# A two-layer block in split precision: the first two weight tiles are split by halves, their products are reordered, and x by token is loaded later

## The chip, the cores and the metric

The kernel runs on one core of a Trainium2 chip. The time is the device time of one execution in microseconds (us), and less is better. The engines are TensorE (PE; its weight loads are listed as PEld), VectorE (DVE), ScalarE (ACT), GpSimd (POOL) and SyncE (SP), which issues nearly all transfers.

## The reference, cut to what matters

The whole program is two transformer-like blocks over 256 tokens of width 2048, all in float32. Only its first step is touched here: a root-mean-square norm of x, and one wide product.

```python
h = rms_norm(x, g_mix_pre[layer])          # x: 256 x 2048
proj = h @ w_in[layer]                     # w_in: 2048 x 9728
aq, ak, av, hq, hf, hi, hg, gate_a, gate_b = jnp.split(proj, split_at, axis=-1)
aq = rotary(aq.reshape(B, S, ATTN_HEADS, ATTN_HEAD_DIM), positions)
```

Everything behind it (windowed attention, a gated recurrence, a feed-forward part, then the second block) works on what comes out of this product.

## The kernel before

**Three products for one.** A float32 product is made of three in the type fp32r: each operand is split into a high part (a copy rounded to fp32r, made by ACT) and a low part (operand minus high part, made by DVE). PE adds up high x high, low weight x high x, and high weight x low x. In the profile the high and low parts of weights are `wh` and `wl` (or `ah` and `al`, when the operand buffers of a later stage are lent for it), those of x by feature are `hh` and `hl`.

**Units, blocks, slots, items.** A unit is a weight of 256 rows by 512 columns (512 KB, 128 x 1024 in the chip's memory: two tiles of 128 x 512). It takes 12 matmuls of 512 columns: two tiles of rows, two halves of the tokens, three products. A block is eight units that add up in one pair of PSUM banks; the blocks `qkv` 0, 1 and 2 are the first three (units 0 to 23). Blocks alternate between two pairs of banks, so block 2 (its first unit is unit 16) can't start before block 0 has been read out of its banks: `unit` waits for `a_ev`, which ACT signals in its stage `q(0)`. An item is one transfer into a landing buffer (`raw` 0 to 3 or four places in `arena`). Units are numbered from 0, and item n is unit n here. A slot is one step of a common timetable, and in slot t PE does unit t.

**What sets the order.** Each engine has a program of its own, written out ahead of time. `drive` walks the slots: in each it does what `AHEAD` has, then the engine's main work (`unit` on PE, `high` on ACT, `low` on DVE), and then lets every stage that `START` has begun go on to its next `yield`, in the order in which they were begun. On DVE, from slot 10 on, the stages come before the main work of the slot. Engines do their lists strictly in order and wait on semaphores. `high` and `low` run ahead of PE: slot 12 of ACT splits units 15 and 16, slot 13 unit 17, slot 14 unit 18.

**The stages that matter here.** `xstats` squares and sums x by token (`X0`, four blocks of 512 columns, two halves of tokens: eight ACT instructions 128 x 512, each followed by a read of its sum), DVE adds the sums up, POOL takes the root, DVE copies it to `R1` and signals `v_r1`. `tables` makes the sine tables for the rotary step (DVE computes angles, ACT takes `Sin`, four times). `lb` prepares a small vector with one `Exp` on ACT. `q(0)` reads block 0 out of its banks on ACT, scaled by `R1` (so it waits for `v_r1`). `Exp` and `Sin` each need an ACT_TABLE_LOAD before them when the table isn't the one loaded.

**Transfers.** SP issues in order: weights (`item`), x by feature (`x_t`, eight pieces of 256 KB), x by token (`x_nat`, four pieces of 512 KB), and three small constants. Units 0 to 7 have buffers of their own from the start.

**The beginning.** PE does 14 matmuls on zeros first. For unit 0 it does its four high products, then the four with the low weight, then the four with low x; unit 1 and all others wait for both low parts before the first matmul.

## Time and profile before

| | |
|---|---|
| time, median of 3 runs | 2183.93 us (2182.58 to 2184.54) |
| time of the profiled execution | 2185.99 us |
| its span in the profile | 2184.2 us |
| mean granted TensorE clock | 0.997 of full speed |
| busy in the span: PE / DVE / ACT / POOL | 2171.8 / 1522.7 / 1109.9 / 47.1 us |
| DMA, mean over the span | 230 GB/s |

The span runs from the first to the last instruction that the profile shows; the profiled execution took 1.8 us more than its span and 2.1 us more than the median. Times inside the trace are counted from the span's start.

### The profile page before, as it was taken

Reading aid. Unit: us, or ns where it says so; the run is one execution under the profiler, and the core shown is the slowest. Engines: PE = TensorE matmul, PEld = TensorE weight load, DVE = VectorE, ACT = ScalarE, POOL = GpSimd, SP = SyncE. Lnnn points to the kernel's source line nnn. Section 1 sums busy time; section 2 is a strip of 40 time slices with the busy share of each in tenths; the row PEclk is TensorE's granted clock in tenths of the full one; section 3 lists DMA queues with packets and bytes.
Section 4 is the critical chain, followed back from the end, with each engine's and each line's share of the span. In section 5 each row is a group of like instructions: output and inputs, shape, how many; then the busy total and the mean of one; then the engine's idle time right before and its main releaser. Section 6 shows DMA issues by size and latency. Waiting matters only on the chain.

```text
span 2184.2 us, 27819 instructions
## 1 busy us (share of the span) xinstructions
PE 2171.8 (99%) x10865; PEld 1799.8 (82%) x10865; DVE 1522.7 (70%) x2026; ACT 1109.9 (51%) x1521; POOL 47.1 (2%) x66
## 2 busy tenths in 40 slices
PE   9999999999999999999999999999999999999999
PEld 7888887888888888888888888887888887888887
DVE  6675479778867777777777778767465577555566
ACT  6676466444446444444443444566465455546452
POOL 0000000100000000000000000000000000000000
PEclk9999999999999999999999999999999999999999
DMA  9544665598886898999999989574564573665573
GB/s 327 169 144 146 193 178 172 173 392 292 281 290 225 300 304 302 311 299 307 305 303 309 305 302 304 180 246 118 146 195 149 165 250 116 172 171 157 156 237 120
DMA packets 243220, 502.87 MB, mean 230 GB/s; under 512 B 17024, under 2 KB 25456, under 8 KB 241936
## 3 DMA queue, kind: packets, MB, share of 16 engines
q1 hardware_dynamic: 239792, 486.20, 68.9%
q0 software_dynamic: 3296, 14.88, 1.9%
q8 instruction: 86, 1.41, 0.3%
q14 instruction: 46, 0.38, 0.1%
HBM read 498.89 MB, written 2.12 MB: 229 GB/s over the span
## 4 chain that ended last, share of the span: by engine, by line
PE 94%; DVE 2%; DMA 2%; ACT 1%; issue 1%; SPq 0%; POOL 0%; DVEq 0%; ACTq 0%
PE bank L959 90%; PE bank L962 4%; ACT arena L1398 1%; DMA raw<-in_w_in 1%; DMA arena<-in_w_in 1%; DVE wl L2015 0%; DMA raw<-in_w_ple_gate 0%; ACT wh L1398 0%; DVE hl L2015 0%; DVE arena L2023 0%; ACT ah L1398 0%; DVE arena L2022 0%; SPq L754 0%; DVE al L2015 0%; SPq L750 0%
## 5 line engine op out<-in xcount | busy, mean ns | idle before, releaser
L1398 ACT ACTIVATE wh<-raw 128x1024 fp32r<-128x1024 f32 (+2 forms) x500 | 520.6, 1043 | 656.1 <-PE bank L959 600.4
L2015 DVE TENSOR_TENSOR wl<-raw,wh 128x1024 fp32r<-128x1024 f32 (+2 forms) x500 | 599.6, 1202 | 343.3 <-ACT wh L1398 341.6
L959 PE MATMUL bank<-wh,hh 128*128 128x512 f32 (+1 forms) x1568 | 617.2, 395 | 4.0 <-DVE wl L2015 3.2
L959 PE MATMUL bank<-wh,hl 128*128 128x512 f32 (+1 forms) x1568 | 605.1, 387 | 0.0
L959 PE MATMUL bank<-wl,hh 128*128 128x512 f32 (+1 forms) x1568 | 604.3, 386 | 0.0
L959 PE MATMUL bank<-wh,ah 128*128 128x512 f32 (+1 forms) x1168 | 456.1, 391 | 0.4 <-ACT ah L1398 0.2
L959 PE MATMUL bank<-wh,al 128*128 128x512 f32 (+1 forms) x1168 | 450.9, 387 | 0.0
L959 PE MATMUL bank<-wl,ah 128*128 128x512 f32 (+1 forms) x1168 | 450.1, 386 | 0.0
L959 PEld LDWEIGHTS bank<-wh,hh 128*128 128x128 f32 x1568 | 294.8, 188 | 63.2 <-DVE wl L2015 4.1
L959 PEld LDWEIGHTS bank<-wh,hl 128*128 128x128 f32 x1568 | 294.2, 188 | 60.5 <-DVE hl L2015 0.5
L959 PEld LDWEIGHTS bank<-wl,hh 128*128 128x128 f32 x1568 | 295.2, 188 | 55.6
L1398 ACT ACTIVATE wh<-arena 128x1024 fp32r<-128x1024 f32 x184 | 195.1, 1061 | 274.2 <-PE bank L959 267.6
L2015 DVE TENSOR_TENSOR wl<-arena,wh 128x1024 fp32r<-128x1024 f32 x184 | 225.0, 1224 | 94.0 <-ACT wh L1398 93.5
L959 PEld LDWEIGHTS bank<-wh,al 128*128 128x128 f32 x1168 | 219.2, 188 | 43.9
L959 PEld LDWEIGHTS bank<-wh,ah 128*128 128x128 f32 x1168 | 219.2, 188 | 43.1 <-issue 1.0
L959 PEld LDWEIGHTS bank<-wl,ah 128*128 128x128 f32 x1168 | 219.5, 188 | 42.0
L2022 DVE SCALAR_TENSOR_TENSOR arena<-arena,ccol 128x768 f32<-128x768 f32 x148 | 149.8, 1012 | 0.0
L2015 DVE TENSOR_TENSOR arena<-arena 128x512 f32<-128x512 f32 (+7 forms) x207 | 101.3, 532 | 16.2 <-ACT arena L1398 15.2
L959 PE MATMUL bank<-arena 128*32 128x32 f32 (+8 forms) x1274 | 106.5, 262 | 2.4 <-DVE arena L2074 1.2
L2022 DVE SCALAR_TENSOR_TENSOR arena<-raw,ccol,arena 128x768 f32<-128x768 f32 x106 | 107.3, 1012 | 0.0
L959 PEld LDWEIGHTS bank<-arena 128*32 128x32 f32 (+3 forms) x1274 | 84.5, 153 | 25.8 <-issue 19.9
L962 PE MATMUL bank<-cst,arena 128*128 128x128 f32 x628 | 92.4, 276 | 2.0 <-ACT arena L1398 1.0
(136 smaller groups left out, 1353.3 us busy)
## 6 DMA issues: line engine op xcount, KB each, us to landing
raw<-in_w_in SPq DMA_DIRECT2D x245, 512.0 KB, 3.8
arena<-in_w_ada SPq DMA_DIRECT2D x148, 384.0 KB, 4.8
arena<-in_w_gate_up SPq DMA_DIRECT2D x97, 512.0 KB, 4.5
raw<-in_w_ada SPq DMA_DIRECT2D x108, 384.0 KB, 4.7
raw<-in_w_out SPq DMA_DIRECT2D x80, 512.0 KB, 4.9
raw<-in_w_gate_up SPq DMA_DIRECT2D x79, 512.0 KB, 4.5
raw<-in_w_down SPq DMA_DIRECT2D x45, 512.0 KB, 5.2
arena<-in_w_down SPq DMA_DIRECT2D x43, 512.0 KB, 5.1
```

The lines of the kernel that those rows point to most:

```text
L959: return i.matmul(o, l, x, start=start, stop=stop, skip_group_check=False)
L962: return i.transpose(o, x, idn)
L1398: return i.activation(o, x, fn, scale=scale, **k)
L2015: return i.tensor_tensor(o, a, b, op)
L2022: return i.scalar_tensor_tensor(out=o, in0=a, scalar=s, in1=b, op0=op0, op1=op1)
```

## The change

Seven things change, all in the first 24 slots.

1. PE does 9 instead of 14 matmuls on zeros (each appears twice in the trace).
2. ACT splits units 0 and 1 in two halves of 128 x 512, with a signal for each half (`a_hik`, then `a_hi`), and DVE takes their low parts by halves too (`v_lowk`, then `v_item`).
3. The first of x's high tiles is made by DVE (`v_hi0`), ahead of everything else that DVE splits, instead of ACT.
4. PE does the products of units 0 and 1 in pairs, each behind a wait for its own operands.
5. SP issues the four `x_nat` pieces two items later: behind items 8, 9, 10 and 11 instead of 6, 7, 8 and 9.
6. `xstats` starts in slot 11 instead of 8, and takes two blocks of columns (four squares) in a slot instead of one, so it ends in slot 12 instead of 11 on ACT.
7. `q(0)` starts in slot 14 instead of 13. `lb` still starts in slot 13.

```diff
@@ -101,7 +101,7 @@
         b.append(Block(name, n, w, row0, nk, n0, nw, ph, pair0, **k))
 
     for n in range(3):
-        add("qkv", n, "w_in", 0, 16, 512 * n, 512, "H1", whole="hwx" if n == 0 else "")
+        add("qkv", n, "w_in", 0, 16, 512 * n, 512, "H1")
...
@@ -390,9 +390,9 @@
...
-    start(8, "xstats")
+    start(11, "xstats")
     start(6, "tables")
-    start(13, "q", 0)
+    start(14, "q", 0)
     start(13, "lb")
     start(19, "q", 1)
...
@@ -768,13 +768,15 @@
                 if n < 8:
                     x_t(n)
                 item(n)
-                if n > 5:
-                    x_nat(n - 6)
+                if n > 7:
+                    x_nat(n - 8)
             i.dma_start(CST[:, 0:K_IF], A["k_cst"]).then_inc(*S.d_cst.dma())
             i.dma_start(SINK, A["attn_sinks"].partition_broadcast(P).rearrange("p a n -> p (a n)")).then_inc(*S.d_sink.dma())
             i.dma_start(GN, A["hgrn_gnorm"].partition_broadcast(P).rearrange("p a n -> p (a n)")).then_inc(*S.d_gn.dma())
             for n in range(10, len(ITEMS)):
                 item(n)
+                if n < 12:
+                    x_nat(n - 8)
...
@@ -797,7 +799,7 @@
             def xstats():
-                yield from range(4)
+                yield from range(2)
                 e.wait_ge(*S.v_rms.at("x"))
                 root(RSTD, SSUM, 2, S.g_rms.up("x"))
 
@@ -980,7 +982,7 @@
             def begin():
                 e.wait_ge(*S.v_zero.at())
                 bk = bank(("keep", 0), S.p_keep, 0)
-                for _ in range(14):
+                for _ in range(9):
                     x = mm(bk[:, 0:P], ZERO[:, 0:P], ZERO[:, 0:P], True, True)
                 x.then_inc(*S.p_keep.up(0))
 
@@ -994,6 +996,42 @@
                 hi, lo = pair_of(bl.ph, bl.pair0 + u)
                 wh, wl = split_at(g)
                 op, first, last = (bl.ph, bl.pair0 + u), u == 0, u == bl.nk // 2 - 1
+                def part(z, q, start=False):
+                    for m in range(2):
+                        ks, ws = slice(m * P, (m + 1) * P), slice(q * nw, (q + 1) * nw)
+                        x = mm(acc[m][:, 0:nw], (lo if z == "x" else hi)[:, q, ks], (wl if z == "w" else wh)[:, ws], start, False)
+                    return x
+
+                if g == 0:
+                    e.wait_ge(*S.a_hik.at(0))
+                    e.wait_ge(*S.v_hi0.at())
+                    part("h", 0, True)
+                    e.wait_ge(*S.v_lowk.at(0))
+                    part("w", 0)
+                    e.wait_ge(*S.a_hi.at(0))
+                    e.wait_ge(*S.a_op.at(*op))
+                    part("h", 1)
+                    e.wait_ge(*S.v_lo0.at())
+                    part("x", 0)
+                    e.wait_ge(*S.v_item.at(ITEM_OF[0]))
+                    part("w", 1)
+                    e.wait_ge(*S.v_op.at(*op))
+                    part("x", 1).then_inc(*S.p_unit.up(0))
+                    return
+                if g == 1:
+                    e.wait_ge(*S.a_hik.at(1))
+                    e.wait_ge(*S.a_op.at(*op))
+                    part("h", 0)
+                    e.wait_ge(*S.a_hi.at(1))
+                    part("h", 1)
+                    e.wait_ge(*S.v_lowk.at(1))
+                    part("w", 0)
+                    e.wait_ge(*S.v_item.at(ITEM_OF[1]))
+                    part("w", 1)
+                    e.wait_ge(*S.v_op.at(*op))
+                    part("x", 0)
+                    part("x", 1).then_inc(*S.p_unit.up(1))
+                    return
...
@@ -1416,7 +1454,14 @@
                         e.wait_ge(*landed(it.place).at(n))
                         if PLACE[g][1] is not None:
                             e.wait_ge(*S.p_unit.at(PLACE[g][1]))
-                        copy(split_at(g)[0][:, 0:w], raw_at(it.place)[:, 0:w]).then_inc(*S.a_hi.up(g))
+                        hi, raw = split_at(g)[0], raw_at(it.place)
+                        if g < 2:
+                            copy(hi[:, 0:512], raw[:, 0:512]).then_inc(*S.a_hik.up(g))
+                            if g == 0:
+                                x_high(0)
+                            copy(hi[:, 512:1024], raw[:, 512:1024]).then_inc(*S.a_hi.up(g))
+                        else:
+                            copy(hi[:, 0:w], raw[:, 0:w]).then_inc(*S.a_hi.up(g))
 
...
@@ -1438,11 +1483,14 @@
             def x_split(p):
+                if p:
+                    x_high(p)
+
+            def x_high(p):
                 hi = pair_of("H1", p)[0]
                 e.wait_ge(*S.get(f"d_xt{p}").at())
-                x = copy(hi[:, 0, :], XT[:, 2 * p, :], scale=XCOL[:, 2 * p:2 * p + 1])
-                if p == 0:
-                    x.then_inc(*S.a_tile.up("H1"))
+                if p:
+                    copy(hi[:, 0, :], XT[:, 2 * p, :], scale=XCOL[:, 2 * p:2 * p + 1])
                 copy(hi[:, 1, :], XT[:, 2 * p + 1, :], scale=XCOL[:, 2 * p + 1:2 * p + 2]).then_inc(*S.a_op.up("H1", p))
 
             def xstats():
@@ -1454,7 +1502,8 @@
                         x = f(JUNK, X0[:, m, c * 512:(c + 1) * 512], ACTF.Square, accum=SS[:, m, c:c + 1])
                         x.then_inc(*S.a_xs.up(c, m))
                         e.wait_ge(*S.a_xs.at(c, m))
-                    yield
+                    if c % 2:
+                        yield
 
...
@@ -2045,6 +2094,14 @@
                         g = it.unit
                         w = 2 * BLK[UNITS[g][0]].nw
                         wh, wl = split_at(g)
+                        if g < 2:
+                            e.wait_ge(*S.a_hik.at(g))
+                            tt(wl[:, 0:512], raw[:, 0:512], wh[:, 0:512].bitcast(F32), ALU.subtract).then_inc(*S.v_lowk.up(g))
+                            if g == 0:
+                                x_low(0, 0).then_inc(*S.v_lo0.up())
+                            e.wait_ge(*S.a_hi.at(g))
+                            tt(wl[:, 512:1024], raw[:, 512:1024], wh[:, 512:1024].bitcast(F32), ALU.subtract).then_inc(*S.v_item.up(n))
+                            continue
                         e.wait_ge(*S.a_hi.at(g))
                         tt(wl[:, 0:w], raw[:, 0:w], wh[:, 0:w].bitcast(F32), ALU.subtract).then_inc(*S.v_item.up(n))
                     else:
@@ -2072,20 +2129,26 @@
             def begin():
                 i.memset(COLS[:, 60:61], 0.0)
                 i.memset(ZERO, 0.0).then_inc(*S.v_zero.up())
+                e.wait_ge(*S.d_xt0.at())
+                then(ts(pair_of("H1", 0)[0][:, 0, :], XT[:, 0, :], XCOL[:, 0:1], None, ALU.mult), S.v_hi0)
+
+            def x_low(p, z):
+                hi, lo = pair_of("H1", p)
+                k = 2 * p + z
+                return stt(lo[:, z, :], XT[:, k, :], XCOL[:, k:k + 1], hi[:, z, :].bitcast(F32), ALU.mult, ALU.subtract)
 
             def x_split(p):
-                hi, lo = pair_of("H1", p)
                 e.wait_ge(*S.a_op.at("H1", p))
-                stt(lo[:, 0, :], XT[:, 2 * p, :], XCOL[:, 2 * p:2 * p + 1], hi[:, 0, :].bitcast(F32), ALU.mult, ALU.subtract)
-                stt(lo[:, 1, :], XT[:, 2 * p + 1, :], XCOL[:, 2 * p + 1:2 * p + 2], hi[:, 1, :].bitcast(F32), ALU.mult,
-                    ALU.subtract).then_inc(*S.v_op.up("H1", p))
+                if p:
+                    x_low(p, 0)
+                x_low(p, 1).then_inc(*S.v_op.up("H1", p))
 
             def mean(n, *key):
 
                 then(ts(SSUM, SSUM, 1.0 / n, EPS, ALU.mult, ALU.add), S.v_rms, *key)
 
             def xstats():
-                yield from range(4)
+                yield from range(2)
                 e.wait_ge(*S.a_xs.at(3, 1))
                 then(red(SSUM, SS, ALU.add), S.v_rms, "x", 0)
                 mean(D, "x")

```

ACT's list, first place: slots 9 to 12 before, slots 11 and 12 after (the rows below begin, before, with the squares of the second block of x, and after with the split of unit 14). `arena,st<-arena 128x512` is a square of x by token, `rope<-arena` a `Sin`, `wh<-raw` or `ah<-arena` 128x1024 the split of one unit. Before:

```order
L1398 ACTIVATE arena,st<-arena 128x512 [waits d_x1]
L1398 ACTIVATE arena,st<-arena 128x512 [waits a_xs]
L1398 ACTIVATE ah<-arena 128x1024 [waits p_unit,d_arena20,a_xs]
L1398 ACTIVATE arena,st<-arena 128x512 [waits d_x2]
L1398 ACTIVATE arena,st<-arena 128x512 [waits a_xs]
L1398 ACTIVATE ah<-arena 128x1024 [waits p_unit,d_arena24,a_xs]
L1398 ACTIVATE rope<-arena 128x64 [waits v_tab]
L1398 ACTIVATE arena,st<-arena 128x512 [waits d_x3]
L1398 ACTIVATE arena,st<-arena 128x512 [waits a_xs]
L1398 ACTIVATE ah<-arena 128x1024 [waits p_unit,d_arena28,a_xs]
```

After:

```order
L1436 ACTIVATE ah<-arena 128x1024 [waits p_unit,d_arena24]
L1436 ACTIVATE rope<-arena 128x64 [waits v_tab]
L1436 ACTIVATE arena,st<-arena 128x512 [waits d_x0,p_keep,a_pre]
L1436 ACTIVATE arena,st<-arena 128x512 [waits a_xs]
L1436 ACTIVATE arena,st<-arena 128x512 [waits d_x1,a_xs]
L1436 ACTIVATE arena,st<-arena 128x512 [waits a_xs]
L1436 ACTIVATE ah<-arena 128x1024 [waits p_unit,d_arena28,a_xs]
```

Before, a pair of squares stood behind each split. Now four stand in one piece between the splits of unit 14 (first row) and unit 15 (last row).

ACT's list, second place: slots 12 to 15 before, slots 12 to 14 after. `arena<-bank,cols` is `q(0)`, the reading of block 0; `arena<-arena 128x16` is the `Exp` of `lb`. Before:

```order
L1398 ACTIVATE ah<-arena 128x1024 [waits p_unit,d_arena28,a_xs]
L1398 ACTIVATE wh<-raw 128x1024 [waits p_unit,d_raw0]
L1398 ACTIVATE wh<-raw 128x1024 [waits p_unit,d_raw1]
L1398 ACTIVATE rope<-arena 128x64 [waits v_tab]
L1398 ACTIVATE arena<-bank0,cols 128x512 [waits v_r1]
L1398 ACTIVATE arena<-bank1,cols 128x512
L1398 ACTIVATE wh<-raw 128x1024 [waits p_unit,d_raw2]
L1398 ACT_TABLE_LOAD
L1398 ACTIVATE arena<-arena 128x16 [waits v_lb]
L1398 ACTIVATE wh<-raw 128x1024 [waits p_unit,d_raw3]
```

After:

```order
L1436 ACTIVATE wh<-raw 128x1024 [waits p_unit,d_raw0]
L1436 ACTIVATE arena,st<-arena 128x512 [waits d_x2]
L1436 ACTIVATE arena,st<-arena 128x512 [waits a_xs]
L1436 ACTIVATE arena,st<-arena 128x512 [waits d_x3,a_xs]
L1436 ACTIVATE arena,st<-arena 128x512 [waits a_xs]
L1436 ACTIVATE wh<-raw 128x1024 [waits p_unit,d_raw1,a_xs]
L1436 ACTIVATE rope<-arena 128x64 [waits v_tab]
L1436 ACTIVATE wh<-raw 128x1024 [waits p_unit,d_raw2]
L1436 ACT_TABLE_LOAD
L1436 ACTIVATE arena<-arena 128x16 [waits v_lb]
L1436 ACTIVATE arena<-bank0,cols 128x512 [waits v_r1]
L1436 ACTIVATE arena<-bank1,cols 128x512
```

Ahead of the two rows `arena<-bank` there are now four more squares, the split of unit 18 (`wh<-raw ... d_raw2`), a table load and the `Exp`; the last three stood behind them before.

SP's list, from the seventh item on (`in_w_in` are weights, `in_x` is x by token, `in_x_t` x by feature). Before:

```order
L758 DMA arena<-in_x 128x2x512
L754 DMA arena<-in_x_t 128x512
L750 DMA arena<-in_w_in 128x2x512
L758 DMA arena<-in_x 128x2x512
L750 DMA raw<-in_w_in 128x2x512 [waits v_item]
L758 DMA arena<-in_x 128x2x512
L750 DMA raw<-in_w_in 128x2x512 [waits v_item]
L758 DMA arena<-in_x 128x2x512
L773 DMA cst<-in_k_cst 128x1022
L774 DMA st<-in_attn_sinks 128x16
L775 DMA st<-in_hgrn_gnorm 128x128
L750 DMA raw<-in_w_in 128x2x512 [waits v_item] x2
```

After:

```order
L750 DMA arena<-in_w_in 128x2x512
L750 DMA raw<-in_w_in 128x2x512 [waits v_item]
L758 DMA arena<-in_x 128x2x512
L750 DMA raw<-in_w_in 128x2x512 [waits v_item]
L758 DMA arena<-in_x 128x2x512
L773 DMA cst<-in_k_cst 128x1022
L774 DMA st<-in_attn_sinks 128x16
L775 DMA st<-in_hgrn_gnorm 128x128
L750 DMA raw<-in_w_in 128x2x512 [waits v_item]
L758 DMA arena<-in_x 128x2x512
L750 DMA raw<-in_w_in 128x2x512 [waits v_item]
L758 DMA arena<-in_x 128x2x512
```

The pieces of `in_x` issued ahead of an item are now 0 instead of 1 for item 7, 0 instead of 2 for item 8, 1 instead of 3 for item 9, 2 instead of 4 for item 10, and 3 instead of 4 for item 11. Ahead of item 12 stand the same transfers in both.

## Rows read from the trace of the kernel before

**Rows 1.** The page: busy us, share of the span, instructions.

```profile
PE 2171.8 (99%) x10865; PEld 1799.8 (82%) x10865; DVE 1522.7 (70%) x2026; ACT 1109.9 (51%) x1521; POOL 47.1 (2%) x66
```

**Rows 2.** Waits of PE, whole span: us in total, times, longest.

```profile
PE bank L959 <- DVE wl L2015: 3.2, 2, 1.7
```

**Rows 3.** Timeline, PE: start us, busy us, instruction, idle time before it and releaser.

```profile
10.77 0.50 PE L959 MATMUL bank<-wh,hh 128*128 128x512 f32 x1 [1.67 <-DVE wl L2015]
...
13.62 0.39 PE L959 MATMUL bank<-wh,hh 128*128 128x512 f32 x1
...
16.34 0.39 PE L959 MATMUL bank<-wh,hh 128*128 128x512 f32 x1
...
37.09 0.50 PE L959 MATMUL bank<-wh,hh 128*128 128x512 f32 x1 [1.55 <-DVE wl L2015]
...
54.43 0.50 PE L959 MATMUL bank<-wh,hh 128*128 128x512 f32 x1 [0.34 <-ACT arena L1398]
...
1845.51 2.06 PE L959 MATMUL bank<-wh,hh 128*128 128x512 f32 x4
```

**Rows 4.** One transfer, item 12 (unit 12), issued at 24.91 us.

```profile
L750 SPq DMA_DIRECT2D arena<-in_w_in x1: 1228/1228/1228, 24.9 to 24.9; - x1
...
DMA to landing us min/median/max: 12.4/12.4/12.4
```

**Rows 5.** Timeline, ACT, 34 to 57 us.

```profile
34.64 1.06 ACT L1398 ACTIVATE wh<-raw 128x1024 fp32r<-128x1024 f32 x1 [4.89 <-DMA raw<-in_w_in]
...
39.12 1.28 ACT L1398 ACT_TABLE_LOAD   x1
41.54 0.26 ACT L1398 ACTIVATE rope<-arena 128x64 f32<-128x64 f32 x1 [1.13 <-DVE arena L2018]
41.70 0.61 ACT L1398 ACTIVATE arena<-arena 128x512 f32<-128x512 f32 x1
...
43.19 1.06 ACT L1398 ACTIVATE ah<-arena 128x1024 fp32r<-128x1024 f32 x1
...
48.38 1.06 ACT L1398 ACTIVATE ah<-arena 128x1024 fp32r<-128x1024 f32 x1
49.35 1.99 ACT L1398 ACTIVATE wh<-raw 128x1024 fp32r<-128x1024 f32 x2
52.83 0.26 ACT L1398 ACTIVATE rope<-arena 128x64 f32<-128x64 f32 x1 [1.49 <-DVE arena L2018]
53.11 1.27 ACT L1398 ACTIVATE arena<-bank,cols 128x512 f32<-128x512 f32 x2
54.27 1.06 ACT L1398 ACTIVATE wh<-raw 128x1024 fp32r<-128x1024 f32 x1
55.34 1.28 ACT L1398 ACT_TABLE_LOAD   x1
56.64 0.22 ACT L1398 ACTIVATE arena<-arena 128x16 f32<-128x16 f32 x1
```

**Rows 6.** Timeline, DVE.

```profile
11.42 1.22 DVE L2015 TENSOR_TENSOR wl<-raw,wh 128x1024 fp32r<-128x1024 f32 x1
...
39.40 1.22 DVE L2015 TENSOR_TENSOR al<-arena,ah 128x1024 fp32r<-128x1024 f32 x1
...
44.35 1.23 DVE L2015 TENSOR_TENSOR al<-arena,ah 128x1024 fp32r<-128x1024 f32 x1 [2.29 <-ACT ah L1398]
...
54.40 0.65 DVE L2018 TENSOR_SCALAR arena<-arena 128x64 f32<-128x64 f32 x3
```

**Rows 7.** Timeline, POOL: the root of the sums of x.

```profile
49.44 0.72 POOL L794 TENSOR_TENSOR st<-st,cst 128x2 f32<-128x2 f32 x1 [34.99 <-DVE st L2018]
```

**Rows 8.** Windows: us, busy us of each engine (instructions), PEclk, DMA share, GB/s.

```profile
34.00:38.00 4.00, 2.45 (x11) 1.72 (x10) 2.09 (x6) 3.30 (x6) 0.00 (x0) 1.00 1.05 389
1838.00:1841.00 3.00, 2.36 (x8) 0.92 (x7) 2.40 (x13) 1.43 (x4) 0.23 (x1) 1.00 0.00 0
1841.00:1848.00 7.00, 7.00 (x21) 4.82 (x20) 6.11 (x14) 5.33 (x9) 0.70 (x1) 0.51 0.00 0
```

## The prediction

> **What bounds the kernel now.** I read the page first: PE is busy 2171.8 of 2184.2 us [rows 1], so a change can win no more than PE's waits (12.4 us in all), and loses whatever it adds to them. Then the waits of PE by releaser: the two longest are both for DVE's low weights, 3.2 us together [rows 2]. The timeline of PE says where [rows 3]: 1.67 us before unit 1 (10.77 us) and 1.55 us before unit 10 (37.09 us). A third, 0.34 us at 54.43 us, is unit 16, released by ACT writing `arena`: that is `q(0)`, which empties the banks that block 2 starts in. A unit takes 2.72 us (16.34 - 13.62), so without waits unit 10 would have started at 13.62 + 8 x 2.72 = 35.4.
>
> Next I read ACT's timeline from 34 to 57 us, as `q(0)` ends it [rows 5]. ACT runs ahead of PE and is not paced by it here: it first sits 4.9 us waiting for unit 10's weights, which land at 34.6, and then works through splits, squares, a table load and sines almost without a pause until it reads block 0 at 53.11 (1.27 us). 53.11 + 1.27 = 54.38, and PE starts unit 16 at 54.43. The reader should see a second deadline behind the first: PE at unit 16 needs two things, its own progress and ACT's list. Before the change the two arrive 0.34 us apart.
>
> **The change, part by part.** *The first units.* Unit 1's weights let ACT finish, and DVE subtract, by halves, and PE starts on the first half, so the 1.67 us before unit 1 should mostly go. But unit 2 then waits: its low part starts on DVE at 11.42 and takes 1.22 [rows 6], and the chain ahead of it (landing of unit 1's weights, two splits on ACT) isn't shortened. Two half copies in place of a whole one can only cost more, by at most another start, which I put at 0.1. So unit 2 starts at about 12.8 instead of 13.62: 0.8 us at PE, not 1.67. Its lower bound is zero gain (everything hidden behind unit 2), its upper 1.67 us.
>
> *Fewer zeros.* The five matmuls fewer end before operands are there, so they win nothing. If PE ran units 0 and 1 at its low clock because of it, 24 matmuls at about 0.5 instead of 0.23 us (2.72 / 12; four take 2.06 in a stretch at the low level [rows 3, 8]) would add up to 6 us to PE ahead of unit 2. The most likely value is 0; what is below hides 4.8 us of it.
>
> *x by token two items later.* Item 12 lands at 24.9 + 12.4 = 37.3 [rows 4], two transfers of 512 KB behind item 10 (34.6 [rows 5]), so one takes 1.35 us. Item 10 has two such pieces fewer ahead of it: it lands at 34.6 - 2.7 = 31.9, is split by 33.0 (1.06) and has its low part by 34.3 (1.22). PE wants it at 12.8 + 0.1 + 8 x 2.72 = 34.7. So the 1.55 us wait goes too. PE would then be 37.09 - 34.7 = 2.4 us ahead. Item 12 has the same bytes ahead of it as before, and still lands at 37.3.
>
> *The squares and q(0), the term that decides.* ACT's list from item 12 on, with durations of the rows of before [rows 5, 6]:
> - 37.3 landing; split of unit 12, 1.06, and 0.1 until DVE starts on it (43.19 + 1.06 to 44.35): 38.5
> - DVE's subtraction and the angles, up to the first sine (39.40 to 41.54), 2.14: 40.6. The table load (1.28) lies inside
> - sine 0.16 (41.54 to 41.70), split of unit 13 1.06, 0.1, then DVE up to the second sine (44.35 to 46.72, taken from its row of before and ACT's chain: subtraction and five small ones) 2.37: 44.3. The split of unit 14 lies inside
> - sine 0.16, four squares. A pair takes 43.19 - 41.70 = 1.49, so 2.98: 47.4
> - splits of units 15 and 16, 0.97 each (48.38 to 49.35): 49.4
> - four squares, 2.98: 52.4
> - split of unit 17, 0.97, sine 0.28 (52.83 to 53.11): 53.6
> - split of unit 18 up to the table load, 1.07 (54.27 to 55.34); load to `Exp`, 1.30 (55.34 to 56.64); `Exp` 0.22: 56.2
> - `q(0)` 1.27, and 0.05 to PE: **57.5**
>
> `v_r1` is ready before that: the last square ends at 52.4, POOL's root takes 0.72 [rows 7], and DVE has unit 17's low part (from 53.5, 1.2) and three small operations (0.65 [rows 6]) behind it at about 55.3; two copies of two columns each, smaller than any of these, are left. `q(0)` is wanted at 56.2. With the rounding of the starts I take 57.4 for unit 16, against 54.43: **+3.0 us**.
>
> Of it, the six instructions put ahead of `q(0)` by moving its start from slot 13 to 14 while `lb` stays (split of unit 18, table load, `Exp`) are 1.07 + 1.30 + 0.22 = 2.6 us. Delaying the squares costs the rest, less what ACT gains by not waiting between them. The term's lower bound: item 12 lands a whole transfer (1.35 us) sooner, which the same bytes ahead of it speak against: +1.7. Its upper bound: DVE is late at a sine or at `v_r1` by one subtraction (1.22): +4.2. I take the sum, nearest to the rows.
>
> PE meanwhile gets to unit 16 early and gains nothing. On its way it waits for unit 13 (low part at 41.9 + 1.2 = 43.1, wanted at 42.9) and about 1.1 us for unit 15, whose split now stands behind four squares (low part at 47.4 + 1.06 + 0.1 + 1.22 = 49.8, wanted at 48.7). It is at unit 16 at 52.6, and waits **4.8 us**. The gain of the first two parts lies wholly inside that wait. Behind unit 16, splits are eight units ahead at most and paced by PE as before, so the shift stays until the end: nothing later in the trace has slack to give back, PE being busy nearly all the time.
>
> The rule of a page speaks on one step. The table load and what follows it cost 1.30 us from row to row, drain included [rows 5]. The Trainium skill ("ScalarE: Activation LUTs", "What ACT_TABLE_LOAD costs") gives about 1.28 us for the load and about 1.38 more for draining, 2.66 for each switch. By it the sum would be 1.4 us more, +4.4; the row shows the load beginning 0.01 us behind the end of the split, and I go by the row.
>
> Against the profiled execution's own 2185.99 us the sum is 2189.0. That execution was 2.1 us over the median of 2183.93, so for the median I say 2183.93 + 3.0 = **2186.9 us**. A measurement of this kernel can tell about 0.2%, 4.4 us, from no change.
>
> **The rivals.**
> - *The clock falls in the new wait.* Before, PE's waits of 1.6 us left it at full clock (34 to 38 us: PE busy 2.45 of 4.00, clock 1.00). But late in the kernel a stretch with few matmuls (8 in 3 us) is followed by 7 us with the granted clock at 0.51, where four products take 2.06 us [rows 3, 8]. That is 1.2 GHz instead of 2.4. The new wait of 4.8 us is longer than any in the trace. Price: if the clock falls in it, up to 7.0 x 0.49 = 3.4 us, and less by what of the low stretch passes while PE waits, so 1 to 3.4 on top of 3.0: +4.0 to +6.4, 2188 to 2190.3. This is the one on the slower side. The Trainium skill ("TensorE: Matmul & The Clock Gate", "Why this matters for your kernels") warns of gaps between bursts of matmuls, which bring the half rate back; by it this case would be the likelier one. The trace shows the fall, and not at what wait it comes.
> - *The gain arrives.* If ACT reads block 0 by 52.6, PE keeps 54.43 - 52.6 = 1.8 us, and up to 3.3 if units 13 and 15 aren't late either (0.3 and 1.1 more, rounded up): 2180.6 to 2182.1. For it: both waits on DVE go. Against: ACT's list is 4.8 us too long, and 2.6 of it is plain work put ahead of `q(0)`. It decides from the point at which `q(0)` ends before 54.4.
> - *Both cancel.* The DMA queue runs better at the start, a sine isn't waited for, and unit 16 starts within 1.5 us of before: 2182.5 to 2185.4.
> - *The table load costs more where it now stands.* 1.4 us more by draining ACT, in front of `q(0)`: 2188.3. The row of before shows no such pause around its load. The page on ScalarE named above has this rule.
> - *The first units don't start earlier* (low clock, or DVE's high tile of x late). It changes nothing at unit 16 and gives the forecast's time; it even shortens the long wait.
>
> **How the numbers follow.** Forecast with the clock kept: 0.43. With the clock fallen: 0.34, about half of it over the bound of 4.4 us. Gain arrives: 0.07. Cancel: 0.13. The dearer table load: 0.03. The range, 2183.6 to 2190.0, holds the first case with its ends (+2.1 to +4.2), nearly all of the second, and half of the fourth. Faster by over 0.2% would need a gain of 4.4 us, more than all waits up to unit 16: 0.02. Slower by over 0.2%: half of the clock case and a little of the forecast's upper end, 0.22. The rest, 0.76, is within 0.2%.
>
> **What would show it.** In the changed kernel's profile: item 10 lands near 32, and no wait of PE before unit 1 or 10. A wait of about 1 us before unit 15. Unit 16 starts near 57.4, released by ACT writing `arena`, after 4 to 5 us. ACT has the table load and `Exp` between the last squares and the two reads of a bank. Granted clock 1.00 from 57 to 65 us, or 0.5 if the first rival holds. I am wrong if unit 16 starts before 54.4, if `q(0)` waits for `v_r1` for over half a microsecond, or if a wait that wasn't there before appears behind unit 16.

## The result, and the profile after

The changed kernel takes 2188.62 us (median of 13 runs, 2188.02 to 2190.63), the kernel before 2184.22 us (13 runs, 2182.58 to 2185.28). The ratio is 1.0021, with a 95% interval of 1.0013 to 1.0030: slower by 4.4 us. The forecast was 2186.9 us, with a range of 2183.6 to 2190.0.

The page of the changed kernel, its span and its first line of engines:

```profile
span 2187.0 us, 27807 instructions
...
PE 2172.2 (99%) x10855; PEld 1800.3 (82%) x10855; DVE 1523.8 (70%) x2029; ACT 1110.2 (51%) x1522; POOL 47.1 (2%) x66
```

PE is busy 0.4 us longer than before [rows 1], and the span is 2.8 us longer. The waits of PE, in the two rows that changed most:

```profile
PE bank L961 <- ACT arena L1436: 5.1, 3, 4.3
...
PE bank L961 <- DVE wl L2064: 0.5, 1, 0.5
```

The two long waits for DVE's low weights [rows 2] are gone, down to 0.5 us. In their place stands one of 4.3 us, and its releaser is ACT writing `arena`, the reading of block 0. PE's timeline says what each unit got:

```profile
12.34 0.50 PE L961 MATMUL bank<-wh,hh 128*128 128x512 f32 x1 [0.54 <-DVE wl L2064]
...
34.25 0.39 PE L961 MATMUL bank<-wh,hh 128*128 128x512 f32 x1
...
48.04 0.50 PE L961 MATMUL bank<-ah,hh 128*128 128x512 f32 x1
...
55.40 0.80 PE L961 MATMUL bank<-wh,hh 128*128 128x512 f32 x1 [4.35 <-ACT arena L1436]
55.99 0.63 PE L961 MATMUL bank<-wl,hh 128*128 128x512 f32 x1
...
60.33 0.40 PE L961 MATMUL bank<-wh,hh 128*128 128x512 f32 x1
60.56 0.40 PE L961 MATMUL bank<-wl,hh 128*128 128x512 f32 x1
```

Read it against [rows 3]. Unit 2 starts at 12.34 instead of 13.62, unit 10 at 34.25 instead of 37.09 without a wait: PE is 2.8 us ahead there. Unit 15 loses a little, at 48.04. Unit 16 starts at 55.40, 1.0 us later than in the first trace of before. And then look at the distances: 0.43 us from one matmul to the next (from 55.99 on), where later ones are 0.23 apart. Unit 16 takes 4.93 us instead of 2.85, so unit 17 comes at 60.33, 3.05 us later than before (54.43 + 2.85 = 57.28). Windows of the same stretch (us, busy of PE, PEld, DVE, ACT, POOL, then PEclk):

```profile
50.00:54.00 4.00, 1.05 (x5) 0.55 (x3) 2.94 (x12) 3.94 (x7) 0.72 (x1) 0.88 0.67 236
54.00:58.00 4.00, 2.60 (x6) 2.12 (x7) 3.76 (x13) 3.98 (x6) 0.76 (x1) 0.50 0.79 231
58.00:62.00 4.00, 4.00 (x15) 3.13 (x15) 4.00 (x6) 3.99 (x6) 1.11 (x2) 0.76 0.54 160
```

The granted clock is at 0.50 from 54 to 58 us, and unit 16 starts at 55.40: in this trace the clock fell in the wait, and the first unit after it runs mostly at 1.2 GHz. Item 12, issued at 24.65 us:

```profile
L750 SPq DMA_DIRECT2D arena<-in_w_in x1: 469/469/469, 24.6 to 24.6; - x1
...
DMA to landing us min/median/max: 10.8/10.8/10.8
```

It lands at 24.65 + 10.8 = 35.5, not at 37.3 as before [rows 4]. From there ACT's list runs as forecast:

```profile
35.50 1.06 ACT L1436 ACTIVATE ah<-arena 128x1024 fp32r<-128x1024 f32 x1 [1.65 <-DMA arena<-in_w_in]
...
38.74 0.26 ACT L1436 ACTIVATE rope<-arena 128x64 f32<-128x64 f32 x1 [0.88 <-DVE arena L2067]
...
42.43 0.26 ACT L1436 ACTIVATE rope<-arena 128x64 f32<-128x64 f32 x1 [1.53 <-DVE arena L2067]
42.59 0.62 ACT L1436 ACTIVATE arena<-arena 128x512 f32<-128x512 f32 x1
...
45.60 1.06 ACT L1436 ACTIVATE ah<-arena 128x1024 fp32r<-128x1024 f32 x1
46.56 1.04 ACT L1436 ACTIVATE wh<-raw 128x1024 fp32r<-128x1024 f32 x1
47.51 0.61 ACT L1436 ACTIVATE arena<-arena 128x512 f32<-128x512 f32 x1
...
50.51 1.06 ACT L1436 ACTIVATE wh<-raw 128x1024 fp32r<-128x1024 f32 x1
51.48 0.24 ACT L1436 ACTIVATE rope<-arena 128x64 f32<-128x64 f32 x1
51.62 1.04 ACT L1436 ACTIVATE wh<-raw 128x1024 fp32r<-128x1024 f32 x1
52.68 1.28 ACT L1436 ACT_TABLE_LOAD   x1
53.98 0.21 ACT L1436 ACTIVATE arena<-arena 128x16 f32<-128x16 f32 x1
54.10 1.25 ACT L1436 ACTIVATE arena<-bank,cols 128x512 f32<-128x512 f32 x2
```

The chain stands in the order of the prediction: split of unit 12 (35.50), two sines that wait for DVE (38.74, 42.43), four squares from 42.59 on, two splits, four squares from 47.51, split, sine, split, table load, `Exp`, and the two reads from 54.10 to 55.35. From landing to PE's start it is 55.4 - 35.5 = 19.9 us. DVE, in the last part of it:

```profile
51.60 1.23 DVE L2064 TENSOR_TENSOR wl<-raw,wh 128x1024 fp32r<-128x1024 f32 x1 [0.32 <-ACT wh L1436]
52.74 0.65 DVE L2067 TENSOR_SCALAR arena<-arena 128x64 f32<-128x64 f32 x3
53.43 0.17 DVE L2157 COPY cols<-st 128x2 f32<-128x2 f32 x1
53.63 0.17 DVE L2067 TENSOR_SCALAR cols<-cols 128x2 f32<-128x2 f32 x1
```

The last row is the signal that `R1` is ready: 53.63 + 0.17 = 53.80, only 0.3 us before ACT takes it.

### The profile page after: what moved, and what is told of

It reads as the page before. It is cut to its first block, busy times and chain, and to the rows that moved or that the text cites. A ratio compares the mean times of both kernels' runs of the same rounds, so it can differ in the third digit from the quotient of the medians.

```text
span 2187.0 us, 27807 instructions
## 1 busy us (share of the span) xinstructions
PE 2172.2 (99%) x10855; PEld 1800.3 (82%) x10855; DVE 1523.8 (70%) x2029; ACT 1110.2 (51%) x1522; POOL 47.1 (2%) x66
## 3 DMA queue, kind: packets, MB, share of 16 engines
HBM read 498.89 MB, written 2.12 MB: 229 GB/s over the span
## 4 chain that ended last, share of the span: by engine, by line
PE 95%; DVE 2%; ACT 1%; DMA 1%; issue 1%; SPq 0%; POOL 0%; DVEq 0%; ACTq 0%
PE bank L961 91%; PE bank L964 4%; ACT arena L1436 1%; DMA raw<-in_w_in 1%; DMA arena<-in_w_in 0%; ACT wh L1436 0%; DVE wl L2064 0%; DVE arena L2072 0%; SPq L750 0%; SPq L754 0%; DVE arena L2071 0%; POOL st L796 0%; DVE hl L2064 0%; DVE arena L2064 0%; ACT ah L1436 0%
## 5 line engine op out<-in xcount | busy, mean ns | idle before, releaser
L1436 ACT ACTIVATE wh<-raw 128x1024 fp32r<-128x1024 f32 (+3 forms) x502 | 521.0, 1040 | 658.0 <-PE bank L961 602.2
L2064 DVE TENSOR_TENSOR wl<-raw,wh 128x1024 fp32r<-128x1024 f32 (+3 forms) x502 | 600.0, 1198 | 341.8 <-ACT wh L1436 340.0
L961 PE MATMUL bank<-arena 128*32 128x32 f32 (+7 forms) x1264 | 104.1, 261 | 2.4 <-DVE arena L2131 1.2
L961 PEld LDWEIGHTS bank<-arena 128*32 128x32 f32 (+4 forms) x1264 | 83.2, 152 | 25.8 <-issue 19.8
```

Of the source, the lines that this page charges most:

```text
L961: return i.matmul(o, l, x, start=start, stop=stop, skip_group_check=False)
L1436: return i.activation(o, x, fn, scale=scale, **k)
L2064: return i.tensor_tensor(o, a, b, op)
```

## The experiments

Each was compared with the kernel before on the same chip; "over before" is the difference of the two medians in one comparison. Times are medians.

**keep_clock: matmuls in the wait.** PE transposes a constant 36 times in the wait, instead of being idle.

```diff
+    ahead(16, "keep", 36, "q0")
...
             def keep(n, key):
+                e.wait_ge(*S.d_cst.at())
                 bk = bank(("keep", key), S.p_keep, key)
```

> The changed kernel with 36 transposes of a constant put on PE ahead of unit 16, in the wait before it (about 4 us of matmuls at full clock). Theory A (the wait before unit 16 costs 1.0 us by itself, and the fall of TensorE's clock in it another 2.1 us): the granted clock stays at 1.00 through unit 16, unit 16 starts at 55.4 to 55.7 and takes 2.85 us instead of 4.9, and the time falls by about 2 us against the changed kernel, to 2186.6 us. Rival B (the low clock is given back later, or isn't what makes the difference): unit 16 is faster, but the time stays at 2188.6 us within 0.7 us.

2187.13 us (11 runs, 2186.07 to 2188.05), ratio 1.0013 (1.0004 to 1.0022). PE's timeline, then the window with PEclk:

```profile
51.01 4.09 PE L965 MATMUL bank<-cst 128*128 128x128 f32 x36
55.52 0.50 PE L962 MATMUL bank<-wh,hh 128*128 128x512 f32 x1 [0.42 <-ACT arena L1438]
```

```profile
52.00:60.00 8.00, 7.58 (x49) 6.55 (x48) 7.62 (x20) 7.94 (x11) 0.84 (x2) 1.00 0.55 168
```

The clock stays at 1.00. Unit 16 starts no sooner (55.52), but unit 17 does: at 58.39, where it was 60.33. The time is 1.5 us below the changed kernel's. The two groups of runs hardly touch (the changed kernel's fastest is 2188.02). The fall of the clock is a real part of the loss, about a third of it; 2.9 us over before are left.

**sched_only: the timetable alone, on the kernel before.**

```diff
-    start(8, "xstats")
+    start(11, "xstats")
-    start(13, "q", 0)
+    start(14, "q", 0)
...
-                    yield
+                    if c % 2:
+                        yield
```

> The kernel before with only the timetable part of the change: squares of x from slot 11 on, two blocks of columns in a slot, and the reading of block 0 in slot 14. Transfers and the first units are those of before. Theory A (ACT's list decides): item 12 still lands at 37.3, the reading of block 0 ends near 57.4, unit 16 starts there instead of at 54.4, and with a fall of the clock in the wait of nearly 4 us the time is 3 to 5 us over before, 2187.2 to 2189.2 us. Rival B (the new order of products or of transfers is what costs): no change against before, 2184.2 us.

2190.42 us (7 runs, 2188.89 to 2191.38), ratio 1.0028 (1.0017 to 1.0039), 6.2 us over before.

```profile
57.95 0.80 PE L959 MATMUL bank<-wh,hh 128*128 128x512 f32 x1 [4.27 <-ACT arena L1398]
```

Item 12 lands at 37.3 here, as the prediction had it, and unit 16 starts 0.55 us behind the 57.4 that it gave. The time is over the range that I expected. The trace says where it goes: unit 16 starts 4.2 us later than in the second trace of before (before_again, below), and takes 5.28 us instead of 2.85, as the granted clock is at 0.50 for nearly all of it (0.71 from 56 to 58 us, 0.50 from 58 to 62). The timetable part alone is slower than the whole change, so in its company the later `x_nat` is a gain; no_start, below, shows that the first units aren't.

**old_sched: the change without its timetable part.** The same edit the other way round, on the changed kernel.

> The changed kernel with the timetable of before: squares from slot 8, one block of columns in a slot, the reading of block 0 in slot 13. The split first units and the later transfers of x stay. Theory A (the gain is real and was lost in ACT's list): item 12 lands at 35.5 instead of 37.3, the list from there to the end of the reading takes 16.3 us as before (38.06 to 54.38), so unit 16 starts at about 51.9 instead of 54.4, with a wait of little over 1 us, too short for the clock: 2.5 us faster than before, 2181.7 us. Rival B (squares of x wait for their later transfers, and the reading comes late all the same): within 1 us of before, 2184.2 us.

2183.26 us (11 runs, 2182.52 to 2184.73), ratio 0.9995 (0.9986 to 1.0004).

```profile
51.91 0.50 PE L961 MATMUL bank<-wh,hh 128*128 128x512 f32 x1 [0.33 <-ACT arena L1436]
```

Unit 16 starts at 51.91, to the tenth as expected, and 3.5 us before the changed kernel. The time falls by 5.4 us against the changed kernel, but only by 0.95 us against before, not by 2.5, and the interval includes no change. That gap is what before_again was for.

**start_only: the first two units alone**, everything else as before.

> The kernel before with only the first two units changed (halves, order of products, 9 matmuls on zeros). Timetable and transfers are those of before. Theory A (a gain at the beginning is lost at the next wait): unit 2 starts 1.2 us earlier, unit 10 still waits for its weights until 37.1, unit 16 starts at 54.4, and the time is that of before, 2184.2 us within 0.5 us. Rival B (what PE wins at the beginning is kept to the end): 1.2 us faster, 2183.0 us.

2184.42 us (11 runs, 2183.04 to 2187.00), ratio 1.0002 (0.9993 to 1.0011): no change.

```profile
36.28 0.50 PE L959 MATMUL bank<-wh,hh 128*128 128x512 f32 x1 [1.13 <-DVE wl L2061]
...
53.63 0.50 PE L959 MATMUL bank<-wh,hh 128*128 128x512 f32 x1 [0.32 <-ACT arena L1434]
```

Unit 2 starts 0.6 us earlier here than in the first trace of before, and unit 10 waits for its weights regardless (1.13 us, released by its low part). Units 10 and 16 start 0.8 us sooner than I expected, but within 0.2 us of the second trace of before (36.44 and 53.78, below). The gain of the beginning is spent at the next wait.

**before_again: a second trace of before.**

> The kernel before, unchanged, for a second trace. Its first profiled execution took 2185.99 us, 1.8 us over the median of its other runs, so the first trace isn't a typical one. Theory A (transfers at the start land up to 0.9 us later in some executions, and the wait before unit 10 passes it on): here item 10 lands near 33.8 instead of 34.6, unit 10 starts near 36.3 and unit 16 near 53.6, and the span is 1 to 2 us shorter. Rival B (the difference comes from late in the kernel, from how long the low clock near 1841 us lasts): unit 16 starts at 54.4 again and the low stretch is shorter.

One execution, 2184.15 us, span 2182.3.

```profile
36.44 0.50 PE L959 MATMUL bank<-wh,hh 128*128 128x512 f32 x1 [0.74 <-DVE wl L2015]
...
53.78 0.50 PE L959 MATMUL bank<-wh,hh 128*128 128x512 f32 x1 [0.32 <-ACT arena L1398]
...
56.64 0.39 PE L959 MATMUL bank<-wh,hh 128*128 128x512 f32 x1
```

Both readings hold in part. Unit 10 starts at 36.44 instead of 37.09, unit 16 at 53.78 instead of 54.43: the transfers were 0.65 us better. The other 1.25 us of the shorter span lie behind that. The granted clock from 1842 to 1850 us is 0.80 here and 0.63 in the first trace. So the first trace of before, on which my sum stood, was late in both places, and against this one the changed kernel starts unit 16 1.6 us later, and unit 17 3.7 us later (60.33 to 56.64).

**nat_only: only x by token later.**

```diff
-                if n > 5:
-                    x_nat(n - 6)
+                if n > 7:
+                    x_nat(n - 8)
...
                 item(n)
+                if n < 12:
+                    x_nat(n - 8)
```

> The kernel before with only the four pieces of x by token moved two items later. Theory A (the gain in old_sched comes from the transfers, by ACT's list starting earlier, and not from the split first units): no wait before unit 10, item 12 lands at 35.5, the reading of block 0 ends near 51.9 and unit 16 starts there: the same time as old_sched, 2183.3 us within 0.5 us. Rival B (the first units' split carries the gain too): 2184.2 us, as before.

2183.29 us (11 runs, 2182.67 to 2184.71), ratio 0.9994 (0.9985 to 1.0003), 1.5 us under before.

```profile
35.39 0.39 PE L961 MATMUL bank<-wh,hh 128*128 128x512 f32 x1
...
51.78 0.50 PE L961 MATMUL bank<-wh,hh 128*128 128x512 f32 x1
```

No wait at unit 10, and unit 16 at 51.78, as in old_sched with its new beginning. What old_sched gains up to unit 16, it gains by the transfers. Against the second trace of before that is 1.9 to 2.0 us, but the medians gain 0.95 (old_sched) and 1.5 (here), and both intervals include no change. Where the rest goes, behind unit 16, isn't settled.

**no_start: the changed kernel with the old beginning.**

> The changed kernel with the first two units as before (14 matmuls on zeros, whole tiles, products in the old order). Theory A (what is won in the first units is spent waiting for the reading of block 0): unit 16 starts at 55.4 as in the changed kernel, its wait about 1 us shorter, and the time is the changed kernel's, 2188.6 us within 0.7 us, or 2 us less if the shorter wait leaves the clock up. Rival B (the first units are a gain in the changed kernel): 1.2 us slower, 2189.8 us.

2189.00 us (11 runs, 2186.62 to 2191.32), ratio 1.0019 (1.0010 to 1.0028), the changed kernel's time.

```profile
55.56 0.62 PE L961 MATMUL bank<-wh,hh 128*128 128x512 f32 x1 [3.81 <-ACT arena L1400]
...
59.99 0.39 PE L961 MATMUL bank<-wh,hh 128*128 128x512 f32 x1
```

Unit 16 starts at 55.56 after a wait of 3.81 us, where the changed kernel waits 4.35. PE comes to the wait 0.7 us later (51.75 instead of 51.05), and most of that is wait that it doesn't have to do. The clock falls all the same (unit 17 is 4.43 us behind unit 16).

**q_first: the reading of block 0 before `lb` again.**

```diff
-    start(14, "q", 0)
+    start(13, "q", 0)
     start(13, "lb")
```

> The changed kernel with the reading of block 0 begun in slot 13 again and ahead of lb, so that the split of unit 18, the table load and Exp stand behind it. Theory A (the scale R1 is late next: DVE copies it only behind unit 17's low part and three table operations, at 53.8): ACT waits for it, reads from 53.8 to 55.1, and unit 16 starts 0.3 us earlier than in the changed kernel, 2188.3 us. Rival B (the 2.6 us of work put ahead of the reading are what costs, as the prediction has it): unit 16 starts near 53 us, and the time is 2.3 to 4 us less, 2184.6 to 2186.3 us.

2189.20 us (11 runs, 2188.42 to 2189.86), ratio 1.0019 (1.0010 to 1.0028): no gain. ACT's timeline:

```profile
51.80 0.24 ACT L1436 ACTIVATE rope<-arena 128x64 f32<-128x64 f32 x1
54.15 1.26 ACT L1436 ACTIVATE arena<-bank,cols 128x512 f32<-128x512 f32 x2 [2.12 <-DVE cols L2067]
```

ACT now waits 2.12 us for DVE's columns (`R1`), and reads from 54.15 on, where the changed kernel did from 54.10. Item 12 landed 0.3 us later in this trace, so by landing the reading is 0.3 us sooner, which is what the first theory expected. The 2.6 us of work taken out of its way only uncover the next one that is late.

**after_again: a second trace of the changed kernel.**

> The changed kernel, unchanged, for a second trace. Theory A (the fall of the clock in the wait before unit 16 happens in every execution, and only its place varies): a wait of 4 to 5 us, unit 16 starting near 55.4, the granted clock at 0.5 for 3.4 to 6.8 us from somewhere between 52 and 57 us, and 1 to 3 us lost by it. Rival B (the first trace happened to catch it): clock at 1.00 through unit 16, and a span 2 us shorter.

One execution, 2187.70 us, span 2185.9.

```profile
55.66 0.50 PE L961 MATMUL bank<-wh,hh 128*128 128x512 f32 x1 [4.34 <-ACT arena L1436]
...
60.12 0.39 PE L961 MATMUL bank<-wh,hh 128*128 128x512 f32 x1
```

```profile
55.60:60.20 4.60, 4.54 (x13) 3.59 (x14) 4.41 (x11) 4.57 (x7) 0.76 (x1) 0.63 0.52 162
```

Again a wait of 4.34 us and a unit 16 of 4.46 us. But here the clock is still at 1.00 from 52.00 to 55.60, in the wait, and at the first matmul behind it (0.50 us, against 0.80 in the first trace), and falls only then. At unit 16, or just ahead of it, the clock fell in all five traces with an idle wait of 3.5 us or more there (both of the changed kernel, sched_only, no_start, q_first), and in none of the others.

**best: unit 16 freed of its second deadline.** On old_sched, DVE makes `R1` in slot 12 without a pause for POOL, and the sine tables begin a slot earlier.

```diff
-    start(6, "tables")
+    start(5, "tables")
...
                 mean(D, "x")
-                yield
                 e.wait_ge(*S.g_rms.at("x"))
```

> old_sched (the split first units and the later transfers of x, with the timetable of before), and in addition the scale R1 made without a pause in slot 12 on DVE, and the sine tables begun one slot earlier, so that the reading of block 0 waits for neither. Theory A (unit 16 is the only deadline that kept the gain from arriving): the reading ends before 51 us, unit 16 follows unit 15 without a wait at about 51.3, 0.5 us before old_sched, and the time is 0.5 us under it, about 2182.8 us, 1 to 2 us under the kernel before. Rival B (another wait takes its place between 30 and 51 us, DVE being held by POOL's root or the earlier angles): no better than old_sched, 2183.3 us.

2182.61 us (11 runs, 2181.42 to 2183.80), ratio 0.9994 (0.9985 to 1.0002), 1.3 us under before.

```profile
51.36 0.39 PE L961 MATMUL bank<-wh,hh 128*128 128x512 f32 x1
```

Unit 16 follows unit 15 without a wait. It has the lowest median here, 5.7 us under the changed kernel by the two differences from before (+4.4 and -1.3), but against the kernel before the interval just includes no change.

**best_old_start: best with the old beginning.**

> The kernel best, with the first two units and the 14 matmuls on zeros of before. Theory A (with no deadline at unit 16, what the first units win is kept to the end): unit 2 starts near 13.7 instead of 12.4 to 12.9, unit 16 near 51.9 instead of 51.3, and the time is 0.6 to 1 us over best. Rival B (the beginning makes no difference in any version, being hidden): the same time as best within 0.3 us.

2183.76 us (11 runs, 2181.93 to 2185.02), ratio 0.9997 (0.9988 to 1.0006), 1.2 us over best. The two intervals overlap, so that the beginning is worth something once nothing waits behind it is likely, not settled. Its trace caught a fall of the clock behind a wait of 1.78 us before unit 1, and thus overstates it (unit 16 at 53.8):

```profile
9.00:12.40 3.40, 1.62 (x7) 1.02 (x7) 2.47 (x4) 3.34 (x6) 0.00 (x0) 1.00 1.03 390
12.40:16.00 3.60, 3.60 (x11) 2.79 (x10) 3.58 (x7) 3.25 (x6) 1.98 (x3) 0.53 1.05 393
```

## Why the prediction was right, point by point

**What bounds, and the second deadline.** Right. The argument that PE at unit 16 needs its own progress and ACT's list, and that the list would decide, is shown by old_sched and sched_only: with the old timetable unit 16 starts at 51.91, with the new one on the old transfers at 57.95, both released by ACT.

**The units on the way.** Unit 13 doesn't wait, and unit 15 loses 0.2 us where I had 1.1, as ACT's list begins 1.8 us sooner there. Neither matters, unit 16 being late anyway.

**The first units.** The direction was right, the size small: unit 2 starts 1.28 us earlier, I had 0.8 (unit 1's weights also landed 0.4 us sooner in that trace; in start_only unit 2 starts 0.6 us earlier). That it gives nothing in the end was right, by start_only and no_start.

**x by token later.** Right that the wait at unit 10 goes. Mis-sized were the landings: item 10 lands at 30.1, not at 31.9, and for "item 12 has the same bytes ahead of it as before, and still lands at 37.3" the trace has 35.5. Part of that is chance: item 12 lands between 36.5 and 37.3 us in the four traces with the old transfers, and between 35.5 and 36.0 in the nine with the later `x_nat`. Equal bytes didn't give equal landing times. The last section says which transfers take the difference; why they do isn't settled.

**The chain of ACT.** The term is landing plus list. The list was forecast at 57.5 - 37.3 = 20.2 us and measured 19.9. Only the landing moved it: unit 16 came at 55.40, not at 57.4, which is +1.0 against the first trace and +1.6 against the second, for a forecast of +3.0. Both are below the lower bound that I gave for this term (+1.7, which the range then took as +2.1).

**Where the term comes from.** Wrong: "the six instructions put ahead of `q(0)` ... are 2.6 us. Delaying the squares costs the rest". With them out of the way (q_first) nothing is won. `R1` is ready at 53.80 and `q(0)` free at 54.10, so both paths are of one length, and both hang on the squares, of which the last ends at 50.4 in the changed kernel and at 45.8 in old_sched. I had put DVE's work ahead of the last two small copies at an end of "about 55.3", against 56.2 for `q(0)`, and should have read from it that taking away 2.6 can't give more than 0.9.

**The clock.** The forecast kept the clock (0.43), and the rival in which it falls had 0.34. The rival is what happened, in both traces of the changed kernel, and its range, 2188 to 2190.3, holds the measured 2188.62. It costs 2.1 us at unit 16 in the first (4.93 for 2.85), 1.6 in the second; keep_clock puts 1.5 us on it in the median. The rule of the Trainium skill that I had weighed ("TensorE: Matmul & The Clock Gate", "Why this matters for your kernels": gaps between bursts bring the half rate back) agrees with the traces here: after the idle waits of 3.5 to 4.4 us before unit 16, or in them, the clock came down every time, and with transposes in the wait it didn't. The waits of 1.67 and 1.55 us in [rows 3] weren't followed by a fall, though one of 1.8 us at the beginning was (best_old_start).

**The dearer table load.** It didn't come. From the load's start to `Exp` it is 53.98 - 52.68 = 1.30 us, as in the trace of before, and the load begins 0.02 us behind the split of unit 18 (51.62 + 1.04). That isn't the 2.66 that the Trainium skill ("ScalarE: Activation LUTs", "What ACT_TABLE_LOAD costs") gives with its drain.

**The sum.** +1.6 us by ACT's list and +1.5 to 2.1 by the clock make +3.1 to +3.7 against the second trace of before; unit 17 shows 3.7, the medians +4.4. The forecast of +3.0 had one of these terms too large and left the other out, and the errors cancel in part. That the forecast is as near as 1.7 us is luck in that measure: its direction and the place of the loss were right, its split of the loss wasn't. The last 0.7 us I can't place. Late in the kernel the clock is low for different lengths in single executions (0.63 and 0.80 from 1842 to 1850 us in the two of before), which is of that size, but no run ties the two together. I had named a new wait of PE behind unit 16 as a sign of being wrong. The changed kernel has one of 0.74 us, for ACT writing `arena`, at 1845.84, that the first trace of before hasn't; the second trace of before has it too, at 1842.19, so the change didn't bring it.

## What to carry to other kernels

When a wait of the bounding engine is removed, look for the next point at which it needs another engine's whole list, and compute when that list is through. Here everything won before unit 16, 2.8 us, was worth nothing, because the list of ACT that unit 16 waits for was made later by the same change. Several works ahead of one signal often end together: taking one away shows the next, so compute all the paths into it, not the longest alone. And a wait on TensorE can cost more than its length, since matmuls behind it run at the low clock: here 1.6 and 2.1 us more after waits of 4.3 us. Transposes of no use in it (36, 4.09 us) gave 1.5 us back.

## What the runs showed that I had not expected

In q_first unit 0 took 5.0 us, at 0.43 us for each matmul, against 3.1 in the trace of the changed kernel, though the profile gives PEclk 1.00: the 12 matmuls of unit 0 fill 5 of these 6 us. Of the seven traces with nine matmuls on zeros it is the only one in which the whole unit was slow (in keep_clock its first two matmuls were), and in the six with 14 none of unit 0 was. Whether the smaller number is the cause isn't shown.

```profile
5.00:11.00 6.00, 5.47 (x16) 4.11 (x15) 5.29 (x11) 4.82 (x10) 0.00 (x0) 1.00 1.00 352
```

The record of the clock seems to begin with its first change, so at the start the distances of the matmuls have to be read instead. It cost nothing there, since the wait before unit 16 took it up.

The 1.8 us by which item 12 lands sooner lie at two small constants. SP issues three in a row: 511 KB (`cst`), then 8 KB, then 64 KB (the row `st` below). The first and the last, with the time from issue to landing, before (issued at 18.91 and 20.83) and in the changed kernel (at 16.21 and 18.16):

```profile
cst<-in_k_cst SPq DMA_DIRECT2D x1, 511.0 KB, 12.4
st<-in_hgrn_gnorm SPq DMA_DIRECT2D x1, 64.0 KB, 12.5
```

```profile
cst<-in_k_cst SPq DMA_DIRECT2D x1, 511.0 KB, 12.2
st<-in_hgrn_gnorm SPq DMA_DIRECT2D x1, 64.0 KB, 10.6
```

So the last lands 2.0 us behind the first before (33.3 and 31.3), and 0.4 us behind it with `x_nat` later (28.8 and 28.4): with a difference of nearly 1.7 us this is most of the 1.8. In the other three traces with the old transfers it is 1.1 to 1.8 us, in all nine with the later `x_nat` 0.4. The large transfers around them keep their distance of about 1.35 us in both. That shows where the time is, not why: no run moves the constants alone.
